# A 16-expert layer's weights loaded by halves of the ring instead of by quarters

## The reference

```python
def _expert_choice_ffn(h, norm_g, w_router, w_gate, w_up, w_down):
    b_, n_, _ = h.shape
    u = _rmsnorm(h, norm_g)
    aff = jax.nn.softmax(jnp.einsum('bnd,de->bne', u, w_router).astype(jnp.float32), axis=-1)
    cap = EC_CAPACITY * n_ // N_EXPERTS            # 2 * 272 // 16 = 34 rows per expert
    g, idx = lax.top_k(jnp.swapaxes(aff, 1, 2), cap)
    xs = jax.vmap(lambda ub, ib: ub[ib])(u, idx)
    hid = (jax.nn.silu(jnp.einsum('becd,edf->becf', xs, w_gate))
           * jnp.einsum('becd,edf->becf', xs, w_up))
    y = jnp.einsum('becf,efd->becd', hid, w_down) * g[..., None].astype(h.dtype)
    return jnp.zeros_like(h).at[jnp.arange(b_)[:, None, None], idx].add(y)
```

## Time and profile before

| | |
|---|---|
| median of three runs | 2233.07 us |
| span of the profiled execution | 2237.3 us (the page gives no other time of this execution) |
| PE busy | 2117.3 us (95%) |
| DVE, ACT, POOL busy | 725.7, 642.1, 42.5 us |
| DMA moved | 725.21 MB, mean 324 GB/s |
| granted clock of PE, mean | 0.995 of full speed |
| experts 1 to 15, by the timeline | 277.8 to 1519.1 us |

### The profile page before, as it was taken

The page is one execution under the profiler, slowest core; times in us unless marked ns, Lnnn a source line. Parts: engine busy times, 40 slices in busy tenths (PEclk is TensorE's granted clock), DMA queues, the critical chain, the costliest instruction groups (busy, mean ns, idle before and its releaser), DMA issues.

```text
span 2237.3 us, 27188 instructions
## 1 busy us (share of the span) xinstructions
PE 2117.3 (95%) x12048; PEld 1298.9 (58%) x12048; DVE 725.7 (32%) x1041; ACT 642.1 (29%) x1024; POOL 42.5 (2%) x73
## 2 busy tenths in 40 slices
PE   9999999999899989999899899989999999999999
PEld 9987443333333333333333333337888998988997
DVE  8983110010010010010010010016665564876553
ACT  6664110010010010010010010005565444965442
POOL 3101000000000000000000000000000000000000
PEclk9999999999999999999999999999999999999999
DMA  7529999999999999999999999997444656544653
GB/s 238 176 96 389 408 403 430 430 425 429 429 426 430 429 426 429 429 425 429 430 424 429 429 426 430 429 422 238 139 169 156 203 188 197 173 158 151 198 189 113
DMA packets 153551, 725.21 MB, mean 324 GB/s; under 512 B 8662, under 2 KB 106378, under 8 KB 127962
## 3 DMA queue, kind: packets, MB, share of 16 engines
q1 hardware_dynamic: 152248, 721.47, 80.7%
q0 software_dynamic: 608, 1.36, 0.2%
q10 hardware_dynamic: 578, 0.64, 0.1%
HBM read 722.38 MB, written 1.07 MB: 323 GB/s over the span
## 4 chain that ended last, share of the span: by engine, by line
PE 59%; DMA 30%; DVE 6%; ACT 3%; issue 1%; SPq 0%; DVEq 0%; ACTq 0%
PE bank L1356 22%; PE bank L1232 17%; DMA weight_ring<-in_w_up_dram 12%; DMA weight_ring<-in_w_gate_dram 9%; DMA weight_ring<-in_w_down_dram 8%; PE bank L1191 5%; PE bank L1314 4%; PE bank L1387 2%; DVE weights_ring L2443 1%; PE bank L1162 1%; PE bank L1048 1%; DVE arena L2503 1%; PE bank L1289 1%; PE bank L1573 1%; PE bank L1596 1%
## 5 line engine op out<-in xcount | busy, mean ns | idle before, releaser
L1232 PE MATMUL bank<-weight_ring,arena 128*64 128x506 f32 x3036 | 644.9, 563 | 34.0 <-DMA weight_ring<-in_w_up_dram 17.8
L1232 PEld LDWEIGHTS bank<-weight_ring,arena 128*64 128x64 f32 x3036 | 213.4, 134 | 425.2 <-issue 384.4
L1314 PE MATMUL bank<-weight_ring,arena 128*64 128x512 f32 x1408 | 323.2, 611 | 64.1 <-DMA weight_ring<-in_w_down_dram 64.1
L2803 DVE SCALAR_TENSOR_TENSOR arena<-arena,bank 128x506 f32<-128x506 f32 (+1 forms) x48 | 28.0, 638 | 913.5 <-ACT arena L2036 913.5
L2835 DVE TENSOR_TENSOR weights_ring<-weight_ring,weights_ring 128x2048 fp32r<-128x2048 f32 x110 | 249.8, 2289 | 126.6 <-ACT weights_ring L2137 126.3
L1314 PEld LDWEIGHTS bank<-weight_ring,arena 128*64 128x64 f32 x1408 | 100.4, 140 | 275.8 <-issue 191.5
L1356 PE MATMUL bank<-input_high,weights_ring 128*128 128x256 f32 x1920 | 248.5, 281 | 0.7 <-issue 0.7
L1356 PEld LDWEIGHTS bank<-input_high,weights_ring 128*128 128x128 f32 x1920 | 234.6, 188 | 3.0 <-issue 2.5
L2137 ACT ACTIVATE weights_ring<-weight_ring 128x2048 fp32r<-128x2048 f32 x109 | 205.6, 1908 | 60.1 <-DMA weight_ring<-in_w_ffn_down_dram 41.0
L1191 PE MATMUL bank<-arena 128*128 128x256 f32 x512 | 142.9, 404 | 0.0
L1191 PEld LDWEIGHTS bank<-arena 128*128 128x128 f32 x512 | 87.3, 189 | 82.6 <-issue 75.6
(11 more groups left out here) (425 smaller groups left out, 1969.6 us busy)
## 6 DMA issues: line engine op xcount, KB each, us to landing
weight_ring<-in_w_down_dram SPq DMA_DIRECT2D x62, 2816.0 KB, 21.7
weight_ring<-in_w_up_dram SPq DMA_DIRECT2D x61, 2816.0 KB, 20.0
weight_ring<-in_w_gate_dram SPq DMA_DIRECT2D x60, 2816.0 KB, 19.3
weight_ring<-in_w_ffn_gu_dram SPq DMA_DIRECT2D x44, 1024.0 KB, 5.1
weight_ring<-in_w_ffn_down_dram SPq DMA_DIRECT2D x22, 1024.0 KB, 4.8
weight_ring<-in_w_in_dram SPq DMA_DIRECT2D x16, 1024.0 KB, 6.3
arena<-in_w_xkv_dram SPq DMA_DIRECT2D x8, 2048.0 KB, 23.4
weight_ring<-in_ab_w_in_dram SPq DMA_DIRECT2D x12, 1024.0 KB, 7.7
```

The source lines that it names most:

```text
L1232: last = pe.matmul(bank[first_bank + c][MPAD * half:MPAD * half + MPAD, 0:(hi - lo) * HF], xs3[:, s, :], rows[:, :, HF * half:HF * half + HF],
L1314: last = pe.matmul(bank[6][MPAD * half:MPAD * half + MPAD, :], hidT[:, at:at + MPAD], W[:, j * D + 512 * half:j * D + 512 * half + 512], s ...
L2803: dve.scalar_tensor_tensor(out=v, in0=v, scalar=1.0, in1=bank[c][:, 0:HF * (hi - lo)], op0=ALU.add, op1=ALU.mult)\
```

## The change

From expert 1 on, gate, up and down weights are loaded four slots at a time (`quad_load`, slots 0 to 3 and 4 to 7, 45056 bytes per partition, 5,767,168 bytes), but for the down weights of the last expert, which stay in pairs and pieces. A load of four slots waits until PE has used all four, and PE waits for all four ahead of the first. The counts follow: a quad raises only the semaphore of its first pair (0 or 2), so pairs 1 and 3 get no more loads after expert 0 until the last expert's down weights, which makes four in all (less one for pair 3, whose up slots of expert 0 lie elsewhere).

```diff
-        B_USES = [(3 * EXP - (s == PAIRS - 1) if s < PAIRS else 1) if s < ESLOTS else 0 for s in range(SLOTS)]
+        B_USES = [((3 * EXP if s % 2 == 0 else 4) - (s == PAIRS - 1) if s < PAIRS else 1) if s < ESLOTS else 0 for s in range(SLOTS)]
 ...
         def pair_landed(eng, e, g, use):
 
-            eng.wait_ge(landed(g), 16 * (A_USES[g] + 3 * e + use - (g == PAIRS - 1)))
+            loads = 3 * e + use if g % 2 == 0 or e == 0 else 4
+            eng.wait_ge(landed(g), 16 * (A_USES[g] + loads - (g == PAIRS - 1)))
 ...
+            def quad_load(name, e, q):
+                sp.dma_start(W[:, 4 * q * DFF:4 * (q + 1) * DFF], rows_of(name, e)[:, 4 * q * DFF:4 * (q + 1) * DFF])\
+                  .then_inc(landed(2 * q), 16)
 ...
             def rest_of_expert(e):
-                for g in range(PAIRS):
-                    sp.wait_ge(S("gate_used"), 8 * e + 2 * g + 2)
-                    pair_load("w_up", e, g)
+                for q in range(2):
+                    sp.wait_ge(S("gate_used"), 8 * e + 4 * q + 4)
+                    quad_load("w_up", e, q)
                 if e % 2 and e + 1 < EXP:
                     sp.wait_ge(S("kv_used"), e + 1)
                     kv_load((e + 1) // 2)
+                if e < EXP - 1:
+                    for q in range(2):
+                        sp.wait_ge(S("up_used"), 8 * e + 4 * q + 4)
+                        quad_load("w_down", e, q)
+                    return
                 for g in range(PAIRS):
                     sp.wait_ge(S("up_used"), 8 * e + 2 * g + 2)
-                    if e == EXP - 1 and g == PAIRS - 1:
+                    if g == PAIRS - 1:
                         last_down_load()
                     else:
                         pair_load("w_down", e, g)
 ...
             for e in range(1, EXP):
-                for g in range(PAIRS):
-
-                    sp.wait_ge(S("down_used"), 8 * e - 8 + 2 * g + 2)
-                    pair_load("w_gate", e, g)
+                for q in range(2):
+                    sp.wait_ge(S("down_used"), 8 * e - 8 + 4 * q + 4)
+                    quad_load("w_gate", e, q)
                 rest_of_expert(e)
 ...
-                    elif s % 2 == 0:
+                    elif s % (4 if e else 2) == 0:
                         pair_landed(pe, e, s // 2, use)
 ...
                     while pairs <= DOWN_SLOT[j] // 2:
-                        pair_landed(pe, e, pairs, 3)
+                        if e in (0, EXP - 1) or pairs % 2 == 0:
+                            pair_landed(pe, e, pairs, 3)
```

## The result

The changed kernel takes 2352.78 us (median of four runs, 2351.16 to 2356.30) against 2232.11: ratio 1.0533, 95% interval 1.0513 to 1.0553. It is slower by 120.7 us. 2328 was forecast, with 2297 to 2372 as the range. On the third the changed kernel was run again: 1.0541 (1.0526 to 1.0555). So runs are compared by their ratios, or by stretches of their traces.

The account below looks back on a forecast made before the run. The DMA stream was taken to set the time between expert 2 and expert 15, with PE having slack. 2233.1 + 82 for the experts' longer path + 13 for the clock = 2328 us; 8-in-10 range 2297 to 2372.

Parts of the forecast that it names:

- rival (C): PE's clock in the experts: drops last through most of the gate half, at every long wait; 2366 us, chance 0.15.
- Expert 1: Gate start to gate start: 90.4 us where before took 79.1, +11.3, as waits begin at once.
- Expert 15: Last expert, whose down loads stay pairs: 80.0 us against 77.6, +2.5.
- The signs named beforehand: In the experts: DMA share some 0.93, 400 GB/s, up waits some 80 us, gate some 60, longest 3.5 to 5, clock 0.95.
- The path without a w_xkv load: Expert period from first gate half's arrival to the next, with two load latencies showing: 86.7 us against 80.4.
- The first term: PE's time for both gate halves, taken from expert 1: 28.74 us.
- I take 2.8, between the two: Latency of a half's load beyond its 13.4 us of data: 2.8 us, between ends of 2.5 and 3.2.
- With a w_xkv load: Period of an expert that also loads w_xkv, stream unbroken from up half 1: 90.4 us against 85.7.
- I take 13, half of 25: Clock drops after PE's longer waits at gate half 0 and up half 1: 13 us, ends 0 and 25.
- (A): Weight loads in the experts: not slower, long rows move faster; put at 2230 us, chance 0.05.
- (B): Weight loads in the experts: latency hidden as DMA reads on, no clock price; 2253 us, chance 0.08.
- The start: Gate half 0 of expert 1 lands near 277.4, PE comes at 277.82: costs nothing, but the cover is thin.

Follow-up runs that it names:

- the third: The third chip used for follow-up runs; the kernel before takes 2239.5 us on it, the changed kernel run again is at ratio 1.0541.
- experiments 1 to 3: Kernel before, loads still by pairs, waits by halves: on both SP and PE 1.0569 (2366.9 us), on PE alone 1.0087, on SP alone 1.0021.
- experiment 4: Kernel before with SP's and PE's waits by halves for gate and up loads alone: 1.0528; for down loads of experts 1 to 14 alone: 0.9999.
- with fill everywhere: Changed kernel with matmuls of no use on PE ahead of every long wait from expert 2 on: ratio 1.0446 to the kernel before.
- the control's profile: Profile of the changed kernel run again unaltered, beside the runs with useless matmuls ahead of waits: ratio 1.0541 to the kernel before.
- the steps cut: Changed kernel with six of eight key/value steps behind the gate slots left out from expert 1 on: ratio 1.0371 to the kernel before.

## Why the prediction was right, and where it was off

**What bounds.** Right. The stream sets the time before, and nothing but the grain of the waits takes it down (experiments 1 to 3).

**The range.** The time lies in the range of 8 in 10, but above the forecast's own 2300 to 2350; it is caught by the part that was there for rival (C). The extra time was 120.7 us where 95 were forecast. So the mechanism was right and two of its terms were too small.

**The path.** Right in its stations as PE walks them. Gate and up carry it and down halves are free (experiment 4). Expert 1 took 90.5 us where 90.4 was worked out, but there two errors cancel: the first term was 1.0 too long, and up half 1 landed 17.1 us after its issue where 16.2 was put. Expert 15 took 79.1 where it was 80.0. The signs named beforehand came near: DMA share 0.93, 387 GB/s (400 or a little more was put), waits of 68.2 us for up loads and 58.2 for gate loads, none over 5.6, clock 0.94. One did not come: the next gate load was to be issued when the DMA had run dry. In experts 2 to 14 it went out 1.1 to 3.6 us before the load ahead of it landed; the place where the DMA ran dry was up half 0.

**Its size.** Too small by 42 us in experts 2 to 14: +68 worked out with the unexplained part, +110.6 measured. Means of the changed kernel's trace, the seven experts without a w_xkv load, stand against the terms of "The path without a w_xkv load":

| step | worked out | measured | with fill everywhere |
|---|---|---|---|
| both gate halves, to the issue of up half 1 | 28.7 | 29.8 | 28.4 |
| load of up half 1 | 16.2 | 16.4 | 16.7 |
| up half 1, hidden rows, down half 0 | 25.6 | 27.1 | 26.2 |
| load of the next gate half | 16.2 | 17.0 | 17.2 |
| sum | 86.7 | 90.3 | 88.4 |

(The last column is the mean of six: in expert 14 PE did not wait for up half 1, so its landing can't be read.)

- The first term was worked out 1.0 too long: the last key/value step stands behind the signal that frees the slot, and expert 1 shows 27.8 (277.77 to 305.55). The clock then took 2.0.
- The step "I take 2.8, between the two" for a load's latency was too small for its use. It was 3.0 to 3.4 for up half 1 and 3.6 to 4.0 for the next gate half (means of two profiles, less 13.4), with single loads from 15.8 to 18.9. These loads were issued before the one ahead had landed, so part of it is that one's tail. The 25 loads of the two profiles that met an empty queue took 15.8 to 17.6, mean 16.5: 3.1 beyond their data, what the lone pair showed; the fit of the Trainium skill (DMA: Bandwidth & Descriptors, anatomy of one DMA), made for another issuing engine, is 2.0 and further off. Why two loads into an empty queue can differ by 1.8 us isn't settled.
- With a w_xkv load: 90.4 worked out, 93.9 measured: 30.1 us to the issue of up half 1 (28.7 worked out), 16.7 for its load (16.2), 47.1 from there to the next gate (45.5). The path was put down as an unbroken stream behind up half 1. A second one is as long: up half 1, a wait for down half 0 (there 18.7 us behind up half 1), down half 0 (9.5), and then the next gate load: 28.2 + 17.2 = 45.4 against 45.5 of stream. Where down half 0 started at the low clock (experts 3, 9 and 13; it also landed 1 us later there) the first part took 31.0 to 31.4 instead of 28.2, and that path was the longer. It is a small part of the miss: in experiment 4's kernel with down loads by pairs PE has no wait for the first down half, and these experts still take 93.2.

**The clock.** "I take 13, half of 25" was too small. The fill gave back 23 us between the gates of experts 2 and 15 with some starts still slow, so the full 25 or more and not its half. All 14 gates behind expert 1 started slow, by 1.6 to 2.4 us (in the control's profile 12 of 14). What the text cited, a kernel in which every stretch behind a wait for data begins slow (the Trainium skill, TensorE: Matmul & The Clock Gate, HAM oscillation), was the better guide here. This case's trace agrees for gate half 0 (14 of 14), and not for every wait: up half 1 started slow in 9 of 15 experts, and up half 0, behind waits of 0.4 to 2.1 us, in none.

**The rivals.** (A), long rows move faster, is dead: 13.37 us a half against 13.40. (B), hidden latency, is dead: the rate fell to 387 GB/s, and loads into an empty queue took 16.5 us for 13.4 of data. (C), double clock cost, came near in its time (2366), but not by its mechanism: of the 46 us by which experts 2 to 14 exceed the 1149.3 worked out, 23 or somewhat more are the clock by the fill, and the rest is put down to the latency and, for a small part, the second path.

**The start** was right: 277.77 against 277.82, with the thin cover holding.

## What to carry to other kernels

A ring in two parcels, loaded and read by the parcel, leaves one parcel's load as the only cover: it stays full only while the reader's time on a parcel, up to the signal that frees it, plus a load's latency fit into that load's time. Here that was 13.4 us for a gate half (15.0 to 16.3 with a slow start) + 3.1 against 13.4, whatever slack the whole loop has. With the steps cut it was 10.9 + 3.1 at full clock, still more than 13.4, and with a slow start 12.3 to 13.5 + 3.1. Being fine on one side, at the freeing or at the start of reading, was enough for nearly all of it. Where the engine's clock falls in a wait, the wait is dearer than its length, and the delay feeds back into when the next place comes free.

## What the runs showed of the hardware

- Rows of 45056 bytes and of 22528 bytes per partition move at the same rate in a full queue (13.37 and 13.40 us for 5.77 MB, 431 and 430 GB/s).
- A load of 5.77 MB that meets an empty queue lands 15.8 to 17.6 us after its issue (25 loads in two profiles of the changed kernel, mean 16.5), 2.4 to 4.2 beyond its data. Issued into an emptying queue it took up to 18.9; some of that is the tail of the load ahead.
- Behind waits of 2.06 to 5.6 us the first twelve matmuls of the gate took 4.2 to 4.96 us instead of 2.60 in the first profile of the changed kernel; in the second two gates, behind 0.91 and 2.07 us, started at full speed. In the kernel before waits of 2.2 us did so only sometimes.
- The same instructions behind the experts took 709 us in one profiled execution and 714 to 721 in the others, at a granted clock of 1.00 in the first and in that of before. That is 0.6 to 1.7% between single executions in a stage that no change touches.
